# Routed experts as plain float32 products of 64-row blocks, with each expert's weights loaded once through a ring of four

## The chip, the core and the metric

The kernel runs on one core of one Trainium2 chip. The metric is the device time of one execution in microseconds. The engines named below are PE (TensorE, with PEld for its weight loads), ACT (ScalarE), DVE (VectorE), POOL (GpSimd) and SP (SyncE, which issues most DMAs); each has its own queue of instructions, and they meet only at semaphores.

## The reference, cut to what matters

512 tokens of 1024 columns run through a first block (an attention mixer, then a mixture of experts, then a norm) and a second block (another mixer and an MLP), all in float32. The change lies in the mixture of experts:

```python
scores = sigmoid(xf @ w_router)                       # 512 x 64
choice = scores + b_router                            # groups limited, then the 6 best experts of a token
gate = scores[chosen] / sum * 2.5
for each expert e, on the rows that chose it:
    hb = silu(xb @ w_exp_gate[e]) * (xb @ w_exp_up[e])   # 1024 -> 256
    yb = (hb @ w_exp_down[e]) * gate                     # 256 -> 1024
routed = sum of a token's six yb
shared = (silu(xf @ w_sh_gate) * (xf @ w_sh_up)) @ w_sh_down
```

There are 64 experts. One expert's three weight arrays take 1 MiB each. The 3072 assignments (512 tokens, six experts each) fall unevenly: counted from the reference's own routing on its inputs, an expert gets 5 to 126 of them, and 13 experts get more than 64.

## The kernel before, in words

The program is a sequence of stages, each with its own block of engine programs. Three of them matter here.

`ffn_front_stage` norms the tokens, stores them as rows in DRAM (`r["h"]`, L1475), turns them with TensorE (`turn`), multiplies by the router, picks experts with a long chain of small DVE operations (L1665 to L1724), counts rows for each expert with a triangular product (L1556), and builds lists that say which token stands in which row of which block. The rows of one expert are padded to whole blocks of 128; a block has one expert. DVE works out the expert of each block (L1707 to L1710) and SP carries that list through DRAM to a row on one partition (L1477 to L1485), from which it reads an expert's number into a register. The shared expert runs in the same stage: `shared_product` (four products of 8 tiles) and the down product at L1572 to L1580. `keep_busy` puts filler products on TensorE.

`expert_stage` loops over the blocks in use; four steps are written out, and the loop body holds four (`steps`, L1871). In step b:

- SP loads the weights of block b's expert into one of two places of `raw` (`gate_up` and `down`, L1911 to L1927), once the place's last contents have been split. Gate and up weights come in two halves A and B of 4 KB a partition and array, the down weights C in 8 KB a partition.
- ACT makes a high part in float32r of each piece (`high`, L2062), DVE the low part (`low`, L2107, in `low_part`, L108). Both go to one of four places, `parts`.
- POOL gathers the next block's rows into `xg` (L1971) and scatters results to `y_rows` (L1982); it copies the index column first (L1967, L1978).
- TensorE turns the rows (`turn_rows`, L2007), and multiplies. `split_product` (L99) makes one float32 product of three float32r products, high by high, high by low and low by high. A block has 24 such products of 512 columns for gate and up, 12 for down.
- ACT applies silu (L2096), DVE multiplies by the up half (L2135), TensorE turns the hidden rows (L2047), and TensorE's `down` runs one step later. ACT copies y (`copy_y`, L2083).

`combine_stage` loads each token's six rows of y again (`load_expert_rows`, L1797), six loads ahead of the two norm gains and six behind them, sums them with the gates (token tile 0 on DVE, the others with diagonal products on TensorE, L2213), adds them to x, and applies two norms, of which the first needs `gain` (L2302) and the second `gain2` (L2305).

Of the kernel before, what the change touches and what calls it, by code (L numbers as in the profile page):

```python
# [43 lines left out]
BLOCKS = S * TOPK // P + E  # L44
# [1323 lines left out]
def ffn_front_stage(g, io, hT, swp, r):  # L1368


# [6 lines left out]
    NB = BLOCKS + 4  # L1377
    PAD = 8 * S
    DOWN_BANK = [0, 2, 4, 6, 1, 3, 5, 7]
    HID_BANK = [1, 3, 5, 7]  # L1380
    LIST_BANK = 6
    raw, xg = r["raw"], r["xg"]
    with g.stage() as st:
        stat = g.sb("ffn_stat", [P, 3, NT], ctx=st)


        small = g.sb("router_rows_hidden", [P, 2 * D], F32R, ctx=st)
        coded = g.sb("coded_blocks", [P, 2, TOPK, 2, NB], F32R, ctx=st)
        sums = g.sb("tri_ones", [P, 2, P], F32R, ctx=st)
        Ar = g.sb("assigned_parts", [P, NT + 1, E], F32R, ctx=st)  # L1390
        br = g.sb("brouter", [P, E], ctx=st)
# [11 lines left out]
        A = g.sb("assigned", [P, NT + 1, E], ctx=st)  # L1403
        cnt = g.sb("counts", [P, 5, E], ctx=st)
        row = g.sb("expert_row", [P, NT, E], ctx=st)
# [4 lines left out]
        be = g.sb("block_expert", [P, E + 2], ctx=st)  # L1410
        lists = g.sb("row_lists", [P, NB], I32, ctx=st)
        lists_f = g.sb("row_lists_f", [P, NB], ctx=st)

        h = raw[:, 0, 0:2, :].rearrange("p a n -> p (a n)").rearrange("p (t d) -> p t d", t=NT)
        w = raw[:, 0, 2, 0:KD * E].rearrange("p (k n) -> p k n", k=KD)
        tmp = raw[:, 0, 2, KD * E:KD * E + NT * TOPK * E].rearrange("p (a e) -> p a e", e=E)

        sw = raw[:, 1]
        blocks = xg.rearrange("p u d -> p (u d)")[:, 0:2 * TOPK * NB].rearrange("p (i k b) -> p i k b", i=2, k=TOPK)
        wp = small[:, 0:2 * KD * E].rearrange("p (a k n) -> p a k n", a=2, k=KD)  # L1420
        rows_hot = small[:, 0:2 * TOPK * P].rearrange("p (i k q) -> p i k q", i=2, k=TOPK)
        hidp = small.rearrange("p (a m s) -> p a m s", a=2, m=2)
        gain = g.mod[:, 0:D]
        shared = g.mod[:, 0:4 * D].rearrange("p (t d) -> p t d", t=NT)
        shift, scale = (g.mod[:, i * D:(i + 1) * D] for i in (3, 4))

        hid = scale.rearrange("p (i s) -> p i s", i=2)
        gate_tmp = scale[:, 0:2 * TOPK * E].rearrange("p (a e) -> p a e", e=E)
# [5 lines left out]
        s_hi = g.sem("ffn_high_ready")  # L1434
        s_lo = g.sem("ffn_low_ready")
        s_hst = g.sem("ffn_h_stored")
        s_sw = [g.sem(f"shared_weights_loaded{i}") for i in range(3)]
        s_swh = g.sem("shared_high_ready")
        s_swl = g.sem("shared_low_ready")
# [3 lines left out]
        s_hh = g.sem("shared_hidden_high_ready")  # L1443
        s_hl = g.sem("shared_hidden_low_ready")
        s_dn = g.sem("shared_down_ready")
        s_wr = g.sem("wrouter_loaded")
        s_wp = g.sem("wrouter_parts_ready")
        s_ld = g.sem("route_loads")
        s_rt = g.sem("router_product_ready")
# [12 lines left out]
        s_bes = g.sem("block_experts_stored")  # L1462
# [3 lines left out]
        def _(sp):  # L1466
            sp.dma_start(gain, bcast_rows(io["g_ffn_norm"], D)).then_inc(s_gain, 16)
            sp.dma_start(w, io["w_router"][0].rearrange("(k p) n -> p k n", p=P)).then_inc(s_wr, 16)
            sp.dma_start(br[:], bcast_rows(io["b_router"], E)).then_inc(s_ld, 16)
            for i, key in enumerate(("w_sh_gate", "w_sh_up", "w_sh_down")):  # L1470
# [7 lines left out]
            sp.wait_ge(s_bes, 16)  # L1478
            sp.dma_start(r["be_row"][:], r["be_dram"].rearrange("b a -> a b")).then_inc(s_bes, 16)
# [3 lines left out]
            sp.wait_ge(s_wp, 2)  # L1483
            sp.wait_ge(s_cr, 1)
            sp.wait_ge(s_bes, 32)  # L1485
            fetch_gate_up(sp, io, r, 0)
            fetch_down(sp, io, r, 0)

            sp.wait_ge(s_swl, 3)
            fetch_gate_up(sp, io, r, 1)  # L1490
# [13 lines left out]
        def _(pe):  # L1504
# [59 lines left out]
            for t in range(NT):  # L1564
                list_rows(t)
# [2017 lines left out]
```

## Time and profile before

| | us |
|---|---|
| median of 3 runs | 2053.2 |
| lowest and highest run | 2051.46, 2054.91 |
| span of the profiled execution | 2048.1 |
| TensorE busy in the span | 1875.5 (92%) |
| DVE busy | 1287.6 (63%) |
| ACT busy | 1028.1 (50%) |
| POOL busy | 660.0 (32%) |

All times in the rows further down are microseconds from the span's start, or nanoseconds where a column says so. Busy time of TensorE is the time in which some product is under way, with ends that are modelled; the products overlap in it. A plain float32 product leaves two records in the trace, a float32r product or a transpose leaves one. The DMA share is the time that packets took over the time of 16 DMA engines, so it can pass 1 a little where packets of two queues overlap.

### The profile page before, as it was taken

What the parts mean: (1) busy time and instruction counts of PE and PEld (TensorE: products, weight loads), DVE (VectorE), ACT (ScalarE), POOL (GpSimd) and SP (SyncE); (2) the same over time, 40 slices, a digit from 0 to 9 for tenths busy, and PEclk for the clock granted to TensorE, in tenths of its full rate; (3) what the DMA queues carried; (4) which work ended last, traced back from release to release, by engine and by line L of the source; (5) the groups of instructions that cost most, each with busy time, mean ns of one, the idle gap of its engine ahead of it and who ended that gap; (6) DMA issues with size and microseconds to landing.
All of it is one profiled execution on the core that took longest, in us unless ns stands there. A gap on an engine that the chain in (4) does not pass through costs nothing. (4 is left out here: it accounts for less than half of the span.)

```text
span 2048.1 us, 28547 instructions
## 1 busy us (share of the span) xinstructions
PE 1875.5 (92%) x8812; PEld 1462.0 (71%) x8814; DVE 1287.6 (63%) x1494; ACT 1028.1 (50%) x1359; POOL 660.0 (32%) x526
## 2 busy tenths in 40 slices
PE   7988998997989999999999956899798879999999
PEld 3774665677868888888888834676465558888887
DVE  4673664446879999999999955564556652333332
ACT  3222444422258888888888833453655432222221
POOL 0896991000026666666666612110011100000000
PEclk9999999998889999999999977998899979999999
DMA  8755552123269999999999954332110023231321
GB/s 303 187 165 165 152 140 66 56 93 119 103 221 367 377 388 370 382 383 379 379 369 371 364 221 125 85 83 58 42 37 21 11 65 111 86 119 62 103 91 73
DMA packets 162992, 373.42 MB, mean 182 GB/s; under 512 B 35611, under 2 KB 72810, under 8 KB 154466
## 3 DMA queue, kind: packets, MB, share of 16 engines
q1 hardware_dynamic: 143954, 328.48, 46.0%
q0 software_dynamic: 18960, 43.91, 6.9%
q8 instruction: 48, 0.79, 0.2%
q14 instruction: 30, 0.25, 0.0%
HBM read 356.19 MB, written 29.23 MB: 188 GB/s over the span
## 5 line engine op out<-in xcount | busy, mean ns | idle before, releaser
L108 DVE TENSOR_TENSOR split_low_half<-exp_raw,split_low_half 128x2048 fp32r<-128x2048 f32 x101 | 230.1, 2290 | 32.7 <-ACT split_low_half L2071 32.7
L108 DVE TENSOR_TENSOR split_high_half<-exp_raw,split_high_half 128x2048 fp32r<-128x2048 f32 x96 | 218.6, 2290 | 27.3 <-ACT split_high_half L2071 27.2
L2071 ACT CAST split_low_half<-exp_raw 128x2048 fp32r<-128x2048 f32 x98 | 186.4, 1917 | 23.9 <-PEq L85 18.5
L102 PE MATMUL ps<-split_low_half,xgT 128*128 128x512 f32 x768 | 188.6, 399 | 3.4 <-DVE xgT L108 3.2
L102 PE MATMUL ps<-split_high_half,xgT 128*128 128x512 f32 x768 | 187.8, 397 | 1.1 <-issue 1.1
L2071 ACT CAST split_high_half<-exp_raw 128x2048 fp32r<-128x2048 f32 x96 | 182.5, 1917 | 2.5 <-PE ps L102 2.2
L102 PE MATMUL ps<-h4T,w_up_parts 128*128 128x512 f32 x768 | 176.8, 393 | 4.1 <-DVE w_up_parts L108 4.1
L102 PE MATMUL ps<-w_down_parts,hidden_parts 128*128 128x512 f32 x768 | 174.4, 390 | 0.0
L102 PEld LDWEIGHTS ps<-h4T,w_up_parts 128*128 128x128 f32 x768 | 146.0, 190 | 34.8 <-ACT w_up_parts L162 4.4
L1971 POOL DMA_INDIRECT xg<-h_rows,row_index x63 | 133.4, 2117 | 109.8 <-issue 82.5
L102 PEld LDWEIGHTS ps<-split_low_half,xgT 128*128 128x128 f32 x768 | 144.2, 191 | 34.4 <-issue 4.0
L102 PE MATMUL ps<-split_low_half,w_parts 128*128 128x512 f32 (+1 forms) x576 | 156.7, 427 | 9.9 <-DVE normed L3130 5.1
L102 PEld LDWEIGHTS ps<-w_down_parts,hidden_parts 128*128 128x128 f32 x768 | 144.2, 188 | 29.8
L102 PEld LDWEIGHTS ps<-split_high_half,xgT 128*128 128x128 f32 x768 | 143.2, 190 | 30.3 <-issue 1.2
L102 PEld LDWEIGHTS ps<-split_low_half,w_parts 128*128 128x128 f32 (+1 forms) x576 | 112.6, 200 | 44.2 <-issue 13.3
L1978 POOL COPY out_index<-row_asg_cols 128x1 uint32 x64 | 136.7, 2136 | 11.1 <-ACT exp_y L2083 11.0
L1982 POOL DMA_INDIRECT y_rows<-exp_y,out_index x64 | 86.4, 1350 | 110.0 <-PE ps L2007 61.4
L102 PE MATMUL ps<-h1T,mix_parts 128*128 128x512 f32 x384 | 104.8, 412 | 6.1 <-DVE mix_parts L108 6.1
L108 DVE TENSOR_TENSOR w_up_parts<-w_up_raw,w_up_parts 128x2048 fp32r<-128x2048 f32 (+1 forms) x19 | 36.9, 1954 | 110.3 <-ACT w_up_parts L167 108.9
L108 DVE TENSOR_TENSOR w_down_parts<-w_down_raw,w_down_parts 128x2048 fp32r<-128x2048 f32 (+1 forms) x19 | 36.8, 1954 | 106.7 <-ACT w_down_parts L167 106.7
L2690 POOL TENSOR_SCALAR sb_sums<-mod 128x1280 f32<-128x1280 f32 x6 | 20.7, 3449 | 255.0 <-ACT mod L3029 255.0
L102 PE MATMUL ps<-split_high_half,exp_hT 128*128 128x512 f32 x384 | 97.9, 405 | 2.8 <-DVE exp_hT L108 2.8
(453 smaller groups left out, 3564.6 us busy)
## 6 DMA issues: line engine op xcount, KB each, us to landing
exp_raw<-in_w_exp_gate SPq DMA_DIRECT2D x130, 512.0 KB, 6.2
exp_raw<-in_w_exp_up SPq DMA_DIRECT2D x130, 512.0 KB, 9.9
exp_raw<-in_w_exp_down SPq DMA_DIRECT2D x64, 1024.0 KB, 9.8
w_up_raw<-in_w_up SPq DMA_DIRECT2D x15, 1024.0 KB, 5.2
w_down_raw<-in_w_down SPq DMA_DIRECT2D x15, 1024.0 KB, 5.1
xg<-in_w_in SPq DMA_DIRECT2D x42, 256.0 KB, 3.3
gate_cols<-in_w_mod POOLq DMA_DIRECT2D x18, 512.0 KB, 4.6
exp_raw<-y_rows SPq DMA_DIRECT2D x9, 1024.0 KB, 14.2
```

The source lines that it names most:

```text
L102: mm = nc.tensor.matmul(out, left[a], right[b], start=start and i == 0, stop=stop and i == 2)
L108: return nc.vector.tensor_tensor(dst, x, high.bitcast(F32), ALU.subtract)
L1971: pool.indirect_dma_start(xg[0:n, u % 2, :], None, r["h"], bass.IndirectOffsetOnAxis(ap=idx[0:n, u % 2:u % 2 + 1], axis=0), bounds_check=S ...
L1978: nc.gpsimd.tensor_copy(oidx[:, u % 2:u % 2 + 1], r["row_asg_cols"][:, bass.ds(b - 4, 1)]).then_inc(s_oi, 1)
L1982: pool.indirect_dma_start(r["y"], bass.IndirectOffsetOnAxis(ap=oidx[0:n, u % 2:u % 2 + 1], axis=0), y[0:n, u % 2, :], None, bounds_check=T ...
L2071: nc.scalar.copy(dst, src).then_inc(s_hi[kind], 1)
L2690: nc.gpsimd.tensor_scalar(su[:], z[:], 0.0, None, ALU.max).then_inc(s_br, 1)
```

## The change

- A block has 64 rows in place of 128 (`ROWS`), and an expert with up to 128 rows has up to two blocks. The list of blocks grows to 112 with 8 spare columns. Every expert has at least one block.
- The 128 partitions of a gathered block hold its 64 rows twice: rows 0 to 63 hold the first 512 columns of the tokens, rows 64 to 127 the last 512. Rows of DRAM are addressed as half rows of 2 KB, for the gather and for the scatter.
- All expert products are plain float32 with 64 stationary columns. Two go to the two halves of the array's columns in turn: out partitions 0 to 63 and 64 to 127. Gate and up take 16 products of 256 columns a block, down takes 4 of 512. There are four turns of the rows and one of the hidden rows.
- The split into high and low parts is gone in the loop and in the front stage. In its place DVE copies pieces A and B, and ACT copies piece C, from the ring to fixed places (`work`), once for each block, at an address that a register gives.
- SP loads each of the 64 experts once, in order, through a ring of four places, `SLOTS`. It no longer reads the block list. It relays each landing to a counter (`s_land`) for which ACT and DVE wait, and it loads expert e + 4 once all blocks of expert e are copied (`r["ends"]`). Experts 0 and 1 are loaded from the start of the front stage, 2 after the last shared down product, 3 right after it.
- The expert of each block reaches its row through a TensorE transpose in place of DRAM. The index columns are copied by DVE in place of POOL, four blocks ahead, into four places.
- The router and the shared expert are plain float32, straight from the loaded weights. All `keep_busy` calls but the first (32 fillers) are gone.
- The combination loads all twelve pairs of y rows ahead of the gains, into the four places of the ring.

```diff
-BLOCKS = S * TOPK // P + E
+ROWS = 64
+BLOCKS = S * TOPK // ROWS + E
+NB = BLOCKS + 8
+SLOTS = 4
...
 def ffn_front_stage, sync
+            fetch_expert(sp, io, r, 0, 0)
             for t in range(NT):
                 sp.wait_ge(s_h, t + 1)
                 sp.dma_start(r["h"][t * P:t * P + P, :], h[:, t, :]).then_inc(s_hst, 16)
-            sp.wait_ge(s_be, 1)
-            sp.dma_start(r["be_dram"], r["be_col"][0:NB, :]).then_inc(s_bes, 16)
...
+            fetch_expert(sp, io, r, 1, 1)
+
+            sp.wait_ge(s_sp, 4)
+            sp.wait_ge(s_dn, 8)
+            fetch_expert(sp, io, r, 2, 2)
...
+            fetch_expert(sp, io, r, 3, 3)
...
 def ffn_front_stage, tensor
                 for k in range(KD):
                     c = k * F + (m % 2) * P
-                    mm = split_product(nc, g.ps[:, HID_BANK[m], :], [swp[:, m // 2, a, c:c + P] for a in range(2)],
-                                       parts_of(hT, k), k == 0, k == KD - 1)
+                    mm = nc.tensor.matmul(g.ps[:, HID_BANK[m], :], sw[:, m // 2, c:c + P], hT[:, k, :],
+                                          start=k == 0, stop=k == KD - 1)
...
             shared_product(2)
+            pe.wait_ge(s_be, 1)
+            nc.tensor.transpose(g.ps[:, EXPERT_BANK, 0:P], be[:], g.ident[:]).then_inc(s_et, 1)
+            list_rows(0)
+            list_rows(1)
             shared_product(3)
-            keep_busy(g, 8, 4)
-            for t in range(NT):
-                list_rows(t)
-            keep_busy(g, 10, 4)
+            list_rows(2)
+            list_rows(3)
...
+def fetch_expert(sp, io, r, e, place):
     for half in range(2):
         for j, key in enumerate(("w_exp_gate", "w_exp_up")):
+            src = io[key][0].rearrange("e (h p k) f -> e h p (k f)", h=2, p=P)
+            sp.dma_start(r["raw"][:, place, half, 1024 * j:1024 * j + 1024],
+                         src[bass.ds(e, 1), half].rearrange("a p n -> p (a n)")).then_inc(r["s_raw"][half][place], 16)
+    src = io["w_exp_down"][0].rearrange("e (k p) n -> e p k n", p=P)
+    sp.dma_start(r["raw"][:, place, 2, :].rearrange("p (k n) -> p k n", k=2),
+                 src[bass.ds(e, 1)].rearrange("a p k n -> p (a k) n")).then_inc(r["s_raw"][2][place], 16)
...
 def expert_stage, sync
+        def relay(kind, u, i):
+            sp.wait_ge(s_raw[kind][u], (32, 32, 16)[kind] * (i + 1))
+            sp.sem_inc(s_land[kind], 1)
+
+        def expert(u, i, last):
+            relay(C, u, i)
+            if not (last and u == SLOTS - 1):
+                for kind in (A, B):
+                    relay(kind, (u + 1) % SLOTS, i + (u + 1) // SLOTS)
+            if not last:
+                blocks = sp.value_load(r["ends"][0:1, bass.ds(SLOTS * i + u, 1)], min_val=1, max_val=BLOCKS)
+                for kind in (A, B, C):
+                    sp.wait_ge(s_cp[kind], blocks)
+                fetch_expert(sp, io, r, SLOTS * i + u + SLOTS, u)
...
 def expert_stage, gpsimd
-            pool.wait_ge(s_xt, b - 1)
-            nc.gpsimd.tensor_copy(idx[:, u % 2:u % 2 + 1], r["row_tok"][:, bass.ds(b, 1)]).then_inc(s_i, 1)
-            pool.wait_ge(s_i, b - 1)
+            pool.wait_ge(s_i, b - 3)
             pool.sem_inc(s_seen, 1)
...
 def expert_stage, tensor
+            for k in range(4):
+                tr = nc.tensor.transpose(g.ps[:, u % 2, k * P:k * P + P], xg[:, u % 4, k::4], g.ident[:])
...
+            pe.wait_ge(s_cp[half], b + 1)
+            w = work[:, place(half, u), :].rearrange("p (j k f) -> p j k f", j=2, k=4)
+            for k in range(4):
+                for n in range(2):
+                    mm = nc.tensor.matmul(g.ps[ROWS * n:ROWS * n + ROWS, 2 + u % 2, 0:F],
+                                          xT[:, u % 2, k, ROWS * half:ROWS * half + ROWS], w[:, :, k, P * n:P * n + P],
+                                          start=half == 0 and k == 0, stop=half == 1 and k == 3)
...
+            for k in range(2):
+                for n in range(2):
+                    c = k * D + n * 512
+                    mm = nc.tensor.matmul(g.ps[ROWS * n:ROWS * n + ROWS, 5 + o, :], hT[:, o, ROWS * k:ROWS * k + ROWS],
+                                          work[:, place(C, u - 1), c:c + 512], start=k == 0, stop=k == 1)
...
 def expert_stage, scalar
+        def down_weights(b, u, first):
+            e = expert_of(act, b)
+            act.wait_ge(s_land[C], e + 1)
+            free_place(act, C, b, first, u)
+            nc.scalar.copy(work[:, place(C, u), :], piece_at(C, e)).then_inc(s_cp[C], 1)
...
+            rows_copied(b + 1, u + 1)
             if not start:
                 copy_y(b, u, first, i)
+            down_weights(b, u, first)
             act.wait_ge(s_ht, b + 1)
+            nc.scalar.copy(hT[:, u % 2, :], g.ps[:, 4, 0:P]).then_inc(s_hc, 1)
...
 def expert_stage, vector
+            e = expert_of(dve, b)
+            for kind in (A, B):
+                dve.wait_ge(s_land[kind], e + 1)
+                free_place(dve, kind, b, first, u)
+                nc.vector.tensor_copy(work[:, place(kind, u), :], piece_at(kind, e)).then_inc(s_cp[kind], 1)
...
 def combine_stage, sync
-        for t in range(2, NT):
-            for j in range(PAIRS):
-                if t >= 3:
-                    sp.wait_ge(s_used, min(TOPK, 2 * j + 2))
-                load_expert_rows(sp, r, yk[t % 3], t, j, s_y[t % 3][j])
```

## Rows read from the trace of the kernel before

**Rows 1.** Busy by stretch: PE, PEld, DVE, ACT, POOL; clock, DMA share, GB/s.
```profile
483.00:576.00 93.00, 80.80 (x425) 73.15 (x425) 71.89 (x169) 27.37 (x61) 4.08 (x3) 0.81 0.38 137
554.00:585.00 31.00, 22.90 (x94) 19.01 (x93) 25.65 (x39) 8.14 (x9) 6.49 (x4) 0.72 0.52 201
576.00:1201.00 625.00, 610.73 (x2952) 512.07 (x2952) 555.62 (x387) 526.01 (x456) 373.92 (x254) 0.98 0.97 355
700.00:1000.00 300.00, 299.78 (x1469) 252.04 (x1468) 273.94 (x193) 258.55 (x223) 190.14 (x128) 1.00 1.02 380
```

**Rows 2.** Who waited for whom, 600 to 1180: total, times, longest.
```profile
ACT split_low_half L2071 <- DMA exp_raw<-in_w_exp_up: 1.3, 2, 0.7
```

**Rows 3.** Waits of SP's own queue, 600 to 1180.
```profile
SPq L1916 <- DVE split_low_half L108: 85.5, 60, 1.7
```

**Rows 4.** Groups by line and shape, whole run: busy us, mean ns, idle before.
```profile
L102 PE MATMUL ps<-split_low_half,xgT 128*128 128x512 f32 x768 | 188.6, 399 | 3.4 <-DVE xgT L108 3.2 <-issue 0.2
L2071 ACT CAST split_low_half<-exp_raw 128x2048 fp32r<-128x2048 f32 x98 | 186.4, 1917 | 23.9 <-PEq L85 18.5 <-PE ps L102 4.1 <-DMA exp_raw<-in_w_exp_up 1.3
...
L330 DVE COPY cond<-silu_c 128x1024 f32<-128x1024 f32 x1 | 0.7, 694 | 0.0
...
L3007 ACT COPY soft_pt<-ps 128x512 f32<-128x512 f32 x12 | 7.0, 579 | 11.1 <-PE ps L2758 11.1
```

**Rows 5.** DMA view, 640 to 1170: queue, packets, MB, share of 16 engines.
```profile
DMA packets 50823, 199.26 MB, mean 376 GB/s; under 512 B 9365, under 2 KB 9365, under 8 KB 43644
...
q1 hardware_dynamic: 40453, 176.71, 89.4%
q0 software_dynamic: 10368, 22.53, 12.0%
```

**Rows 6.** DMA view of 0 to 40, then of 1205 to 1238.
```profile
DMA packets 7176, 14.48 MB, mean 362 GB/s; under 512 B 1551, under 2 KB 2136, under 8 KB 6920
...
DMA packets 4291, 13.39 MB, mean 406 GB/s; under 512 B 246, under 2 KB 1137, under 8 KB 4290
```

**Rows 7.** Timeline of PE, line L1127: start, us, what, records.
```profile
242.75 0.66 PE L1127 MATMUL ps<-win_raw,v_mla 128*64 128x128 f32 x8
...
254.12 1.10 PE L1127 MATMUL ps<-win_raw,v_mla 128*64 128x128 f32 x16
```

**Rows 8.** Timeline of PE, line L2776, one half of the columns.
```profile
1444.02 0.87 PE L2776 MATMUL ps<-soft_pt,values 128*64 128x128 f32 x6
...
1458.82 1.09 PE L2776 MATMUL ps<-soft_pt,values 128*64 128x128 f32 x8
```

**Rows 9.** Timeline of the front stage: last score, shared down, first weight split.
```profile
520.03 0.22 ACT L1602 ACTIVATE scores<-ps 128x64 f32<-128x64 f32 x1 [4.90 <-PE ps L102]
...
560.05 11.45 PE L102 MATMUL ps<-split_low_half,router_rows_hidden 128*128 128x512 f32 x48
...
575.91 1.90 ACT L2071 CAST split_low_half<-exp_raw 128x2048 fp32r<-128x2048 f32 x1 [18.48 <-PEq L85]
```

**Rows 10.** Timeline of the loop's end and of the combination.
```profile
1185.61 1.91 ACT L2071 CAST split_high_half<-exp_raw 128x2048 fp32r<-128x2048 f32 x1
...
1190.42 4.60 PE L102 MATMUL ps<-split_high_half,exp_hT 128*128 128x512 f32 x12 [2.77 <-DVE exp_hT L108]
...
1198.24 0.91 POOL L1982 DMA_INDIRECT y_rows<-exp_y,out_index  x1 [1.74 <-issue]
...
1201.44 3.38 SPq L1797 DMA_DIRECT2D exp_raw<-y_rows  x6
1204.86 1.28 SPq L2194 DMA_DIRECT2D final_gain<-in_g_final  x1
...
1220.99 1.29 DVE L2302 SCALAR_TENSOR_TENSOR x<-x,final_stat,final_gain 128x1024 f32<-128x1024 f32 x1 [0.99 <-DMA final_gain<-in_g_final]
...
1227.33 7.13 PE L2213 MATMUL ps<-yk,gate_diagonals 128*128 128x512 f32 x16 [0.22 <-DMA yk<-y_rows]
...
1235.56 1.29 DVE L108 TENSOR_TENSOR split_low_half<-ps,split_low_half 128x512 fp32r<-128x512 f32 x2 [4.56 <-ACT split_low_half L2248]
```

More of the change, by code:

```diff
@@ L1577, in _ @@
                     col = k * D + n * 512
-                    mm = split_product(nc, g.ps[:, DOWN_BANK[c], :], parts_of(hidp, k, t * P, t * P + P),
-                                       [swp[:, 0, a, col:col + 512] for a in range(2)], k == 0, k == 1)
+                    mm = nc.tensor.matmul(g.ps[:, DOWN_BANK[c], :], hid[:, k, t * P:t * P + P], sw[:, 2, col:col + 512],
+                                          start=k == 0, stop=k == 1)
                 mm.then_inc(s_dn, 1)
@@ L1654, in _ @@
             link(v.reciprocal(stat[:, 1, :], stat[:, 2, :]))
-            rows(0)
-            rows(1)
-            rows_low(0)
-            rows(2)
-            rows_low(1)
-            rows(3)
-            rows_low(2)
-            rows_low(3)
-            shared_low(0)
+            for t in range(NT):
+                rows(t)
             dve.wait_ge(s_ld, 16)
@@ L1900, in used_blocks, with expert_of, piece_at @@
     def used_blocks(eng):
-        return eng.value_load(r["n_col"][0:1, 0:1], min_val=24, max_val=BLOCKS)
-    def rhs_of(piece, k):
-        return [parts[piece][:, a, k * 512:k * 512 + 512] for a in range(2)]
+        return eng.value_load(r["ends"][0:1, E - 1:E], min_val=E, max_val=BLOCKS)
+    def expert_of(eng, b):
+        return eng.value_load(r["be_row"][0:1, bass.ds(b, 1)], min_val=0, max_val=E - 1)
+    def piece_at(kind, e):
+        return raw[:, bass.ds(e & (SLOTS - 1), 1), kind, :].rearrange("p a n -> p (a n)")
@@ L1946, in _ @@
+        used = used_blocks(sp)
+        relay(A, 0, 0)
+        relay(B, 0, 0)
+        with sp.Fori(0, E // SLOTS - 1) as i:
+            for u in range(SLOTS):
+                expert(u, i, False)
+        for u in range(SLOTS):
+            expert(u, E // SLOTS - 1, True)
+        sp.wait_ge(s_cp[A], used + 1)
+        sp.wait_ge(s_cp[B], used + 1)
+        sp.wait_ge(s_cp[C], used)
         sp.wait_ge(s_st[0], ((used + 1) >> 1) * 16)
         sp.wait_ge(s_st[1], (used >> 1) * 16)
-        for t in range(2):
+        for t in range(NT):
@@ L2019, in down @@
         def down(b, u, first, i=0):
-            pe.wait_ge(s_hi[C], b)
-            pe.wait_ge(s_lo[C], b)
-            pe.wait_ge(s_hh, b)
-            pe.wait_ge(s_hl, b)
-            if not (first and u == 1):
-                pe.wait_ge(s_y, b - 1)
-            for n in range(2):
-                for k in range(2):
-                    mm = split_product(nc, g.ps[:, 5 + n, :], [hT[:, (u - 1) % 2, a, k, :] for a in range(2)],
-                                       rhs_of(place(C, u - 1), 2 * k + n), k == 0, k == 1)
+            pe.wait_ge(s_cp[C], b)
@@ L2031, in down @@
+            pe.wait_ge(s_hc, b)
+            if not (first and u < 3):
+                pe.wait_ge(s_y, b - 2)
+            o = (u - 1) % 2
+            for k in range(2):
[3 more added lines that the diff above has]
+                                          work[:, place(C, u - 1), c:c + 512], start=k == 0, stop=k == 1)
             mm.then_inc(s_piece, 1)
@@ L2041, in step @@
             gate_up(b, u, 1)
-            turn_rows(b + 1, u + 1, i, False)
+            turn_rows(b + 1, u + 1, i, first and u == 0)
             if not (first and u == 0):
@@ L2168, in combine_stage @@
     s_gain = [g.sem(f"final_gain_loaded{i}") for i in range(2)]
-    s_y = r["s_y"] + [[g.sem(f"y_loaded2{j}") for j in range(PAIRS)]]
+    s_y = r["s_y"]
     s_diag = g.sem("gate_diagonals_ready")
@@ L2360, in moe_and_mixer2 @@
-            r["row_asg_cols"] = g.sb("row_asg_cols", [P, BLOCKS + 4], U32, ctx=c)
-            r["row_tok"] = g.sb("row_tok", [P, BLOCKS + 4], I32, ctx=c)
-            r["s_raw"] = [[nc.alloc_semaphore(f"expert_{n}_loaded{i}") for i in range(2)]
+            r["raw"] = g.sb("exp_raw", [P, SLOTS, 3, 2048], ctx=c)
+            r["y_buf"] = g.sb("exp_y", [P, 2, D // 2], ctx=c)
+            r["be_row"] = g.sb("be_row", [1, NB], I32, ctx=c)
+            r["ends"] = g.sb("expert_ends", [P, E], I32, ctx=c)
```

406 lines of the change are left out of this document (127 added, 279 removed).

## The prediction

> **What bounds the kernel now.** I began with busy times by stretch. The change touches three: the routed front of the mixture (483 to 576 us), the expert loop (576 to 1201) and the combination (1201 to about 1264). The loop is 30% of the span, and in it TensorE is busy 610.7 of 625 us and the DMA engines 0.97 [rows 1]; inside it, from 700 to 1000 us, the two stand at 299.8 of 300 and 1.02, with 380 GB/s moved. Both are full, so I asked who waits for whom. ACT, the first reader of a loaded weight, waits 1.3 us for DMA in 580 us [rows 2], while SP, which issues the loads, waits 85.5 us on one line alone for DVE to free a buffer [rows 3]. So TensorE sets the pace (64 blocks from 576 [rows 9] to 1195 [rows 10], 9.7 us a block), and DMA just keeps up: it is a second limit that lies directly under the first. That is the whole case: taking work from TensorE, ACT and DVE can win only what lies between the two, plus what the new loading order adds.
>
> The profiled span is 2048.1 us and the median of the runs 2053.2 us (2051.46 to 2054.91), so some 5 us lie around the span. I sum differences on the span and take them off the median.
>
> **Blocks.** Counted from the reference's own routing on its inputs, 13 experts have over 64 rows, none over 128 and none has no row. So 64 blocks become 64 + 13 = 77, and the loads stay 64 experts: before, one expert's weights a block (and one extra load), after, one an expert.
>
> **TensorE per block.** Before: 36 products of 512 columns a block at 188.6 / 768 = 0.246 us [rows 4], 8.8 us, and ten transposes. After: plain float32, where one product leaves two records. A 512-column product costs 2 x 7.13 / 16 = 0.89 us in the combination [rows 10]. Whether two 64-column products in the two halves run at once decides everything. The trace has it: at L1127 values of two heads alternate between the halves; 8 and 16 records of 128 columns take 0.66 and 1.10 us [rows 7], 0.22 us for every four records, that is for one product in each half. L2776 works on one half only: 6 and 8 records take 0.87 and 1.09 us [rows 8], 0.22 us for one product. So the pair costs what one costs. Per block: eight pairs of 256 columns at 0.44 and two of 512 at 0.89, 5.3 us; five transposes at 0.11 (a record of [rows 8]), 0.55; two changes between halves and the whole array. No row prices that change by itself: the 8 records of [rows 7] take 0.66 where the slope gives 0.44, so filling and change are at most 0.22 us together, at least nothing; I take 0.15. Together 6.2 us.
>
> **ACT, DVE and POOL per block.** ACT copies the down weights (1.92 [rows 4]), the turned rows and y (0.58 each by the 128x512 copy of [rows 4]) and does two small operations, about 0.7 together by the 128x512 row as an upper bound: 3.8 us. New is that it reads a register from SBUF ahead of the weight copy; the nearest row is POOL's gap of 1.74 us, where it reads one and branches [rows 10], so 0 to 1.74. Behind that load are queued the weight copy and the hidden copy, for which the down product waits: down 1.8, y 0.6, register 0 to 1.7, copy 1.9, hidden copy 0.4 make a loop of 4.7 to 6.4 us. DVE copies 2048 columns twice; the 1024-column copy took 0.69 [rows 4], so at most 1.4 each, and with the product, two index copies and a register 3.5 to 5.2 us. POOL loses its two index copies to DVE. So a block takes 6.2 to 6.5 us and 77 take 477 to 500, against 619.
>
> **DMA becomes the bound.** The loop has 64 x 3.146 = 201.3 MB of weights. Two experts are fetched during the front, where the share is 0.38 [rows 1]; the third waits for the shared expert's last product. So 62 x 3.146 = 195.0 MB remain, and 3072 rows of 4 KB in and out, 25.2 MB: 220.2 MB. Rows move in pieces of 2 KB now, weights all in 4 KB. The rate: 380 GB/s inside the loop [rows 1], 376 over 640 to 1170, at which the two queues' shares add up to 1.01 [rows 5]. The ends are 362 at the kernel's start, with mostly 2 KB pieces and no indirect transfer, and 406 in the combination, 4 KB pieces with no indirect transfer [rows 6]. I take 380, the same mixture of queues: 579 us, with 608 and 542 as ends. The ring of four keeps at least two experts on order while a slot is freed, so I charge no gap. Against 579, compute of 500 and some 10 us of start is hidden, and has 579 / 77 = 7.5 us a block before it shows.
>
> The Trainium skill, "DMA: Bandwidth & Descriptors", Specifications, gives an HBM limit per core of about 358 GB/s, which speaks against this change: 220.2 MB would take 615 us and nearly all the gain would be gone. The 380 and 406 of the two stretches stand against it, so it has no place in the sum; a rate near it is the rival of slower transfers, priced from rows.
>
> **The front.** Removed: the low parts on DVE, the high parts on ACT, a third of the router's records, and the trip of the block list through DRAM. Added: plain products on TensorE, where one (0.89) replaces three of 0.246, so the 16 shared down products take 14.2 us for 11.45 [rows 9]; wider block lists on DVE (120 for 92 columns); the wait of the list product for the expert row. The last score comes at 520.0, and from there a chain of small DVE operations is unchanged. I expect the last score 8 us earlier, 1 us less in the counting, and 5 given back on TensorE, some of it at the lower clock since filler products go: the last shared product ends near 567.5 instead of 571.5. Bounds: 0 to 10 us earlier. The four gathers at its end (POOL) replace two and lie beside those products.
>
> **Start and end of the loop.** Loads run from 567.5, the last lands at 567.5 + 579 = 1146.5. Then the old tail from the last weight copy to the loads of y, 1185.6 to 1201.4, 15.8 us [rows 10], shortened by a down product of 1.8 for 4.6 and a y copy of half the width, 13 us: y is asked for at 1159.5 instead of 1201.4, 41.9 earlier.
>
> **The combination.** All twelve loads of y (12.6 MB) now go out ahead of the final gain, where six did. Before, the gain was issued at 1204.9, and DVE's first use was at 1221.0, after a wait for it [rows 10]. After, 12.6 MB and the gain at 406 GB/s land 32.5 us after the first load for 19.5 before. TensorE's sums hid part of this: DVE's first low part came at 1235.6, 34.1 us in, after them; after, gain, two norms and a turn put it about 41 us in. Cost 7 us (0 to 13).
>
> **Sum.** -41.9 + 7 = -35 on 2053.2: 2018 us. With the rate between 370 and 395 GB/s, 2000 to 2035.
>
> **Rivals.**
> Faster transfers: with ACT and DVE reading less and weights in long runs, the rate reaches the combination's 406: 37 us less, 1981. Against it: indirect transfers stay, in twice as many pieces.
> Slower transfers: 2 KB pieces bring the rate to 362: 29 us more, 2047.
> The clock (the slower end): TensorE waits for weights in every expert, its granted clock falls between 2.4 and 1.2 GHz, and compute becomes the bound. With TensorE at 22.9 of 31 us busy, the clock was 0.72 from 554 to 585 [rows 1]. At 0.72 a block takes 5.85 / 0.72 + 0.3 = 8.4 us, 77 take 649, and with start and tail y is asked for at 1239: 38 + 7 later, 2098. It decides from (1201.4 - 7 - 13 - 571) / 77 = 7.9 us a block on. Against it: once compute is late TensorE no longer waits, and busy it has 1.00 [rows 1]; so it should settle near 7.5 to 8. The Trainium skill, "TensorE: Matmul & The Clock Gate", The HAM clock gate, has the half rate as the default that activity lifts; the 0.72 agrees, and no run here shows the clock under just these gaps.
> The halves don't run together (the change doesn't do what it says): a block takes 5.3 more, 11.5 us, 77 take 886, 2340. The records of [rows 7] speak against it, though at 128 columns, not 256 or 512.
>
> **How the numbers follow.** Chances: forecast 0.52; faster transfers 0.15; slower transfers 0.12; clock or another compute bound over 7.5 us 0.17, a fifth of it still faster; halves one after the other 0.04. A measurement of this kernel tells about 0.2%, 4 us. Faster: 0.52 + 0.15 + most of 0.12, and 0.03, 0.77; same 0.05; slower 0.18. The range takes in most of the fast and slow transfers and a mild compute bound: 1985 to 2060.
>
> **What would show it.** Right: ACT and DVE idle before weight copies with DMA as releaser; DMA share about 1 from 570 to 1146; TensorE busy about 480 of 590; one 64-column product per 0.44 us at 512 columns on average; the first DVE norm waiting for the gain. Wrong: SP waiting for copies while DMA falls under 0.9 (compute bound); records of both halves in single file; a granted clock under 0.9 in the loop; a rate off 370 to 395.

## The result and the profile after

The changed kernel takes 2062.0 us (median of 6 runs, 2057.7 to 2065.5) and the kernel before 2052.8 us (6 runs, 2051.1 to 2055.4): a ratio of 1.0051, 95% interval 1.0029 to 1.0074. The forecast was 2018 us, with a range up to 2060. The change costs 9 us where it should have brought 35, and the time is just above the range. All medians and ratios here leave out three executions that ran far longer than the rest: one of the kernel before (10347 us) and two of `gains_early` (2310 and 3172 us).

First busy time by stretch (columns as in [rows 1]) of the changed kernel:

```profile
576.00:700.00 124.00, 107.70 (x698) 57.25 (x696) 44.40 (x80) 56.03 (x79) 40.21 (x31) 0.93 0.84 317
...
700.00:1000.00 300.00, 261.68 (x1669) 143.94 (x1667) 102.89 (x184) 130.77 (x185) 90.13 (x75) 0.92 0.93 358
...
1000.00:1100.00 100.00, 85.68 (x536) 48.84 (x532) 30.81 (x56) 40.22 (x58) 25.36 (x23) 0.90 1.02 401
1100.00:1200.00 100.00, 86.58 (x549) 47.26 (x549) 35.79 (x65) 44.64 (x62) 28.71 (x23) 0.92 0.72 277
```

In [rows 1] TensorE and DMA were both full from 700 to 1000. Now neither is: TensorE 262 of 300, DMA 0.93, ACT 131 and DVE 103 (259 and 274 before). When no engine is full, the time lies in waits between them. These are the waits from 570 to 1240 (total, times, longest), of DVE:

```profile
DVE work_places L2009 <- SPq L1846: 261.5, 42, 9.1
```

and of SP's own queue:

```profile
SPq L1856 <- ACT work_places L1976: 372.2, 60, 14.2
...
SPq L1846 <- DMA exp_raw<-in_w_exp_up: 5.1, 2, 2.6
SPq L1846 <- DMA exp_raw<-in_w_exp_down: 2.5, 1, 2.5
```

L1846 is the relay: SP adds one to the counter `s_land` when a weight has landed. DVE waits 261.5 us for the relay, and SP at the relay waits 7.6 us for landings in all (5.1 and 2.5). So DVE waits for weights that are there. SP spends 372 us in front of L1856, the wait until all blocks of an expert are copied, which stands in its program ahead of the next relay. In the kernel before, ACT waited for DMA itself [rows 2], and SP's wait was the one for a free buffer [rows 3]; no signal went through SP.

The steps tell it most plainly. From one silu (L1993) to the next there are 76 steps: 49 take 6.4 us (the first of them 5.0), and 27 take 10.4 to 13.1, together 128 us over 6.41 each. One late step and the ordinary one behind it, from the timeline (start, duration; idle before and its releaser in brackets):

```profile
1042.42 1.90 ACT L1976 COPY work_places<-exp_raw 128x2048 f32 x1 [0.33 <-issue]
...
1044.56 0.34 SPq L1734 DMA_DIRECT2D exp_raw<-in_w_exp_gate  x1
...
1045.29 0.28 ACT L1993 ACTIVATE exp_sig<-ps 128x128 f32<-128x128 f32 x1 [0.80 <-PE ps L1923]
...
1045.86 1.94 PE L1938 MATMUL ps<-work_places,exp_hT 128*64 128x512 f32 x8
...
1046.47 0.40 SPq L1737 DMA_DIRECT2D exp_raw<-in_w_exp_down  x1
...
1047.40 2.37 DVE L2009 COPY work_places<-exp_raw 128x2048 f32 x2 [7.80 <-SPq L1846]
...
1049.69 0.27 DVE L2019 TENSOR_TENSOR exp_h<-ps,exp_sig 128x128 f32<-128x128 f32 x1
...
1050.02 0.33 PE L1954 MATMUL ps<-ident,exp_h 128*128 128x128 f32 x1 [2.22 <-DVE exp_h L2019]
...
1050.70 5.16 PE L1923 MATMUL ps<-work_places,xgT 128*64 128x256 f32 x32 [0.36 <-issue]
...
1055.90 0.28 ACT L1993 ACTIVATE exp_sig<-ps 128x128 f32<-128x128 f32 x1 [4.98 <-PE ps L1923]
...
1056.48 1.94 PE L1938 MATMUL ps<-work_places,exp_hT 128*64 128x512 f32 x8
...
1058.35 0.33 PE L1954 MATMUL ps<-ident,exp_h 128*128 128x128 f32 x1
...
1058.60 3.67 PE L1923 MATMUL ps<-work_places,xgT 128*64 128x256 f32 x32
```

Read it as one chain. ACT's copy of the down weights ends at 1044.32. SP waited for that, and issues the five loads of a later expert from 1044.56 to 1046.87. Only then come the relays, and DVE's copies for the next block start at 1047.40, though the load of those weights was issued from 1027.42 on and a load of this kind landed 8.6 us after its issue in the median from 1000 to 1100. DVE works in program order, and the product of the present block (L2019) stands behind these copies. Its input was ready at 1045.57; it starts at 1049.69. TensorE, done at 1047.80, waits 2.22 us, and after that its 32 records take 5.16 us instead of 3.67. The granted clock says why:

```profile
1050.00:1056.00 6.00, 5.62 (x34) 3.57 (x35) 1.65 (x4) 1.02 (x3) 1.67 (x2) 0.72 1.03 414
1056.00:1062.00 6.00, 6.00 (x45) 3.19 (x44) 1.12 (x4) 3.42 (x5) 1.69 (x2) 1.00 1.02 408
```

From 1050 to 1056, behind the wait, it is 0.72, a mixture of 1.2 and 2.4 GHz; from 1056 to 1062, with TensorE busy without a gap, 1.00. So this step of 10.6 us (1045.29 to 1055.90) is 6.4, plus 2.3 for the late hidden rows (4.16 us from the start of the down product to their transpose, against 1.87), 0.4 until the next product starts (0.68 against 0.25), and 1.5 at the lower clock.

The other two stages of the changed kernel: the front's last score, its last shared products and DVE's first copy (with SP's last issue of the front between), and the combination's loads with the first norm that waits for the gain, and the first weight split of the next stage.

```profile
508.12 0.22 ACT L1584 ACTIVATE scores<-ps 128x64 f32<-128x64 f32 x1 [1.12 <-PE ps L1507]
...
547.78 13.90 PE L1567 MATMUL ps<-exp_raw,mod 128*128 128x512 f32 x32
...
566.58 0.49 SPq L1737 DMA_DIRECT2D exp_raw<-in_w_exp_down  x1
...
569.98 3.50 DVE L2009 COPY work_places<-exp_raw 128x2048 f32 x3 [5.14 <-SPq L1846]
...
1205.15 17.17 SPq L1744 DMA_DIRECT2D exp_raw<-y_rows  x12
...
1240.01 1.28 DVE L2180 SCALAR_TENSOR_TENSOR x<-x,final_stat,final_gain 128x1024 f32<-128x1024 f32 x1 [16.21 <-DMA final_gain<-in_g_final]
...
1277.19 1.99 ACT L2822 CAST w_parts<-xg 128x1024 fp32r<-128x1024 f32 x2 [1.71 <-PEq L88]
```

and that first weight split in the kernel before:

```profile
1264.70 1.99 ACT L2948 CAST w_parts<-xg 128x1024 fp32r<-128x1024 f32 x2 [1.73 <-PEq L85]
```

The ledger in the two profiled executions (2048.1 and 2063.7 us, 15.6 apart): the first weight copy 5.9 us earlier (575.91 in [rows 9], 569.98 now), the loop from there to the first load of y 9.6 us longer (625.5 and 635.2), the combination up to the next stage's first split 8.8 us longer (1264.70 less 1201.44 = 63.3, and 72.0). That is 12.5; the remaining 3.1 lies in later stages, which the change doesn't touch. The profiled execution of the changed kernel was the slowest of its six, so the two profiles lie further apart than the medians (9 us).

### The profile page after: what moved, and what is told of

The parts are those of the page before. It is cut to its first block and busy times, and to the rows that moved or that the text cites. A ratio compares the mean times of both kernels' runs of the same rounds, so it can differ in the third digit from the quotient of the medians.

```text
span 2063.7 us, 29262 instructions
## 1 busy us (share of the span) xinstructions
PE 1814.0 (88%) x9192; PEld 1226.4 (59%) x9192; DVE 935.8 (45%) x1480; ACT 772.1 (37%) x1290; POOL 473.7 (23%) x424
## 5 line engine op out<-in xcount | busy, mean ns | idle before, releaser
L2009 DVE COPY work_places<-exp_raw 128x2048 f32 x156 | 189.9, 1243 | 382.9 <-SPq L1846 261.5
L1923 PE MATMUL ps<-work_places,xgT 128*64 128x256 f32 x2464 | 329.9, 427 | 11.2 <-issue 8.8
L1923 PEld LDWEIGHTS ps<-work_places,xgT 128*64 128x64 f32 x2464 | 208.7, 154 | 109.6 <-issue 38.1
L105 PE MATMUL ps<-mix_hT,w_parts 128*128 128x512 f32 (+1 forms) x576 | 159.8, 432 | 9.8 <-DVE normed L3004 5.0
L1976 ACT COPY work_places<-exp_raw 128x2048 f32 x77 | 146.4, 1901 | 25.4 <-issue 25.4
L1938 PE MATMUL ps<-work_places,exp_hT 128*64 128x512 f32 x616 | 150.8, 610 | 3.1 <-ACT exp_hT L1999 3.1
L105 PEld LDWEIGHTS ps<-mix_hT,w_parts 128*128 128x128 f32 (+1 forms) x576 | 113.1, 201 | 46.2 <-issue 13.9
L1884 POOL DMA_INDIRECT xg<-h_rows,row_index x74 | 88.8, 1200 | 47.7 <-DVE out_index L2022 26.4
L1993 ACT ACTIVATE exp_sig<-ps 128x128 f32<-128x128 f32 x77 | 21.4, 278 | 190.3 <-PE ps L1923 190.3
L105 PEld LDWEIGHTS ps<-h1T,mix_parts 128*128 128x128 f32 x384 | 70.0, 194 | 29.0 <-issue 8.2
L1984 ACT COPY exp_y<-ps 128x512 f32<-128x512 f32 x77 | 45.1, 586 | 107.7 <-PE ps L1938 107.7
```

What stands on the lines that cost most here:

```text
L105: mm = nc.tensor.matmul(out, left[a], right[b], start=start and i == 0, stop=stop and i == 2)
L1884: pool.indirect_dma_start(xg[:, u, :], None, h_halves, bass.IndirectOffsetOnAxis(ap=idx[:, u:u + 1], axis=0), bounds_check=2 * S - 1, oob_ ...
L1923: mm = nc.tensor.matmul(g.ps[ROWS * n:ROWS * n + ROWS, 2 + u % 2, 0:F], xT[:, u % 2, k, ROWS * half:ROWS * half + ROWS], w[:, :, k, P * n: ...
L1938: mm = nc.tensor.matmul(g.ps[ROWS * n:ROWS * n + ROWS, 5 + o, :], hT[:, o, ROWS * k:ROWS * k + ROWS], work[:, place(C, u - 1), c:c + 512], ...
L1976: nc.scalar.copy(work[:, place(C, u), :], piece_at(C, e)).then_inc(s_cp[C], 1)
L1984: nc.scalar.copy(y[:, o, :], g.ps[:, 5 + o, :]).then_inc(s_y, 1)
```

## The experiments

Theory S: SP's program order makes landed weights late. Theory D: the loop is at the limit of the transfers, as the DMA share of 1.02 from 1000 to 1100 suggests. Theory R: the ring of four is too short. All kernels below are the changed kernel with the edit that is shown. "Late" counts steps over 6.6 us in the profiled execution, with what they take over 6.41 in all; "y" is the start of the first load of y there.

| kernel | median us | ratio to before, 95% | late steps, us over | y |
|---|---|---|---|---|
| changed kernel | 2062.0 | 1.0029 to 1.0074 | 27, 128 | 1205.2 |
| relay_ahead | 2003.0 | 0.9718 to 0.9796 | 26, 67 | 1144.4 |
| relay_before_issue | 2004.4 | 0.9720 to 0.9797 | 40, 69 | 1145.4 |
| half_weights | 2081.9 | 1.0098 to 1.0180 | 27, 151 | 1225.5 |
| few_bytes | 2064.4 | 1.0036 to 1.0074 | 29, 124 | 1201.1 |
| ahead_few_bytes | 1932.8 | 0.9377 to 0.9455 | 0, 0 | 1073.9 |
| gains_early | 2053.3 | 0.9985 to 1.0031 | 27, 124 | 1196.6 |
| ahead_gains | 1997.2 | 0.9699 to 0.9750 | 27, 70 | 1146.6 |
| one_half | 2331.0 | 1.1309 to 1.1402 | 75 of 11.6, one of 8.5 | 1474.2 |
| ahead_down_long | 1994.0 | 0.9686 to 0.9769 | 25, 62 | 1136.4 |
| ahead_more_copies | 2004.2 | 0.9756 to 0.9807 | 27, 67 | 1146.0 |

### Relays one expert earlier

```diff
-            relay(C, u, i)
             if not (last and u == SLOTS - 1):
+                relay(C, (u + 1) % SLOTS, i + (u + 1) // SLOTS)
+            if not (last and u >= SLOTS - 2):
                 for kind in (A, B):
-                    relay(kind, (u + 1) % SLOTS, i + (u + 1) // SLOTS)
+                    relay(kind, (u + 2) % SLOTS, i + (u + 2) // SLOTS)
             if not last:
                 ... wait for the copies of expert 4 i + u, issue its place's next load
... (ahead of the loop: the relays of expert 0, and A and B of expert 1)
```

> Three theories for the loop of the changed kernel, in which 49 of 76 steps take 6.4 us and 27 take 10.4 to 13.1, 128 us over in all. Theory S (the queue of SP): SP passes on the landing of a weight to the counter that DVE and ACT wait for, but in its program this stands behind the wait for the copies of the expert before and behind five DMA issues, so weights that have long landed are copied late. Theory D (transfers): DMA share 1.02 from 1000 to 1100 us says that the loop already runs at the rate of the transfers, and late steps are steps that wait for them. Theory R (ring): four places are too few. Here SP passes landings on one expert earlier, ahead of the wait for copies and the issues; nothing else changes. S expects the late steps to go until the transfers are the limit: 220.2 MB at 390 to 400 GB/s from 562 us and a tail of 13 give loads of y at 1125 to 1140 in place of 1205, a time of 1982 to 1997. D and R expect 2055 to 2065, as the transfers and the places are the same.

2003.0 us: 59 us less, with the same transfers and the same ring. D and R as the cause of the changed kernel's time fall. Two stretches:

```profile
580.00:700.00 120.00, 119.97 (x846) 63.82 (x840) 54.90 (x94) 65.19 (x94) 48.65 (x37) 1.00 0.97 377
...
700.00:1000.00 300.00, 267.56 (x1802) 147.87 (x1800) 113.55 (x196) 140.83 (x200) 100.55 (x80) 0.97 1.02 402
```

and SP's waits from 570 to 1140:

```profile
SPq L1846 <- DMA exp_raw<-in_w_exp_up: 259.4, 105, 3.8
SPq L1857 <- ACT work_places L1979: 66.2, 20, 9.8
```

The pair of waits has changed places: at the relay SP now waits 259.4 us for landings (5.1 before) and 66 instead of 372 us for copies. Up to 700 us TensorE is full, and DMA moves 377 GB/s; from 700 on DMA is full, at 402. This is the loop that the prediction described. S had expected 1982 to 1997, from 390 to 400 GB/s all the way; the 26 steps that are still late begin at 724 us, in the part where transfers set the pace.

The gain over the changed kernel doesn't come evenly. Counted by steps, relay_ahead leads by 55 us after 52 of the 76 (993 us in the changed kernel) and by 56 after 68 (1131 us). Between these the changed kernel moves as much as relay_ahead (401 GB/s from 1000 to 1100), so there the late relay, that of the step read above too, costs nothing beyond what the transfers take anyway; its price is paid before.

### Relays behind the wait, but ahead of the issues

```diff
             if not last:
                 ... wait for the copies of expert 4 i + u
+            ... the relays, as in relay_ahead
             if not last:
                 fetch_expert(sp, io, r, SLOTS * i + u + SLOTS, u)
```

> As the kernel that passes landings on earlier, but they keep their place behind the wait for the copies and go only ahead of the five issues, which take SP about 2.5 us (1044.56 to 1046.87). S in its narrow form (the issues alone make the landing late): the copy at 1047.40 would begin near 1044.9, and the hidden rows, late by 2.3 us, would be in time, so nearly all late steps go: 1985 to 2020. S in its wide form (the wait itself is too late): late steps shrink to half, 2020 to 2045. D and R: 2055 to 2065.

2004.4 us, the same as with relays ahead of the wait. So the narrow form holds: it is the five issues, 2.3 to 3.0 us on SP in the late steps, that made the relay cost so much, and the wait itself adds little. Up to 720 us, where transfers set no pace yet, delays of 0.4 to 1.0 us remain in six steps; that the transfer-bound part then hides them is not shown by a run of its own. The Trainium skill, "DMA: Bandwidth & Descriptors", Issuing engines are not separate DMA queues, says that the sequencer's time to start a DMA is usually small beside the DMA itself. The trace agrees, some 2.6 us for 3.1 MB, which take about 8 us at 402 GB/s; but it was in the way of the relay, and that cost 59 us.

### Fewer bytes, twice, and once more with earlier relays

```diff
-    sp.dma_start(r["raw"][:, place, ...], src[bass.ds(e, 1), ...])
+    sp.dma_start(r["raw"][0:64, place, ...], src[bass.ds(e, 1), 0:64, ...])          # half_weights
+    sp.dma_start(... [:, :, 0:64], src[bass.ds(e, 1), :, :, 0:64] ...)               # few_bytes, down weights only
```

> The changed kernel with half the bytes for each weight loaded in the loop (60 experts): 64 of 128 partitions are loaded, so the other half holds old weights and the result is another; the number of DMAs, the waits and all the copies and products stay. S expects the time to stay within 10 us of 2062, because no late step waits for bytes. D expects 119 MB in place of 214 MB to end the late steps, with compute of 77 times 6.41 us as the limit: y asked for near 1075, a time of about 1930. R expects a gain of the same kind, because landings come sooner after a place is free.

2081.9 us, 20 more than the changed kernel, where S had within 10 of it. The run didn't separate the theories as meant: the bytes halved, but the packets took nearly the same time. It shows something else. The stretch from 1000 to 1100 us:

```profile
1000.00:1100.00 100.00, 80.03 (x475) 48.18 (x473) 29.96 (x55) 39.36 (x57) 25.92 (x22) 0.87 0.94 205
```

and the first and the last of five issues on SP's timeline:

```profile
790.42 0.52 SPq L1734 DMA_DIRECT2D exp_raw<-in_w_exp_gate  x1
...
792.99 0.64 SPq L1737 DMA_DIRECT2D exp_raw<-in_w_exp_down  x1
```

The five issues take SP 3.2 us here (790.42 to 793.63), and 3.2 in the mean of the 27 late steps, in place of 2.6 in the changed kernel; the 27 late steps are 0.85 us longer each (151 us in place of 128). SP waits 6.5 us for landings at the relay, so the weights are there in this kernel too. More time on SP goes with longer late steps, a dose of the suspected cause, though not the one that was planned; 0.6 us more came out as 0.85, and where the rest comes from is open.

> The changed kernel (relays in their place) with a load of the down weights in the loop that brings 64 of 1024 columns, so the result is another; every DMA, wait, copy and product stays. Half the partitions halved the bytes but not the time of the packets (DMA share 0.94 at 205 GB/s), so that run said little of theory D. Here all 128 partitions stay and an expert brings 2.16 MB in place of 3.15. S: 27 late steps as before, time within 8 us of 2062. D: the late steps go, 1930 to 1960.

2064.4 us, 29 late steps. A third of the bytes less changes nothing: D falls a second time, now with a cut that did thin out the transfers, also from 1000 to 1100 us, where the changed kernel had 1.02 and 401 GB/s:

```profile
700.00:1000.00 300.00, 261.85 (x1679) 146.68 (x1677) 104.73 (x186) 130.90 (x185) 89.71 (x74) 0.92 0.73 263
1000.00:1100.00 100.00, 83.73 (x522) 45.27 (x519) 30.40 (x59) 42.34 (x60) 26.86 (x24) 0.90 0.79 285
```

> The same cut of bytes on the kernel that passes landings on one expert earlier. Its late steps (26, 67 us over 6.41 in all) begin where the slack between landing and copy is 0.3 us, so they should be waits for transfers: 62 times 2.16 MB and 25.2 MB of rows at 402 GB/s are 396 us, less than 77 times 6.41 = 494. If so, nearly all steps take 6.4 us and the time falls by about 65 us, to 1935 to 1942. If SP's queue still holds them, it stays within 20 us of 2003.

1932.8 us, just under the 1935 to 1942 that were expected, and no late step at all. The row of 600 to 1050:

```profile
600.00:1050.00 450.00, 450.00 (x3160) 238.21 (x3160) 209.37 (x353) 246.81 (x352) 187.25 (x141) 1.00 0.90 331
```

TensorE is busy 450.00 of 450 at clock 1.00. So compute alone is 6.41 us a step, and in relay_ahead the transfers are the limit, 70 us above compute in y.

### One half of the array's columns

```diff
-    nc.tensor.matmul(g.ps[ROWS * n:ROWS * n + ROWS, 2 + u % 2, 0:F], ...)
+    nc.tensor.matmul(g.ps[0:ROWS, 7 if n else 2 + u % 2, 0:F], ...)
... (the start and stop flags to match, and the same for the down product)
```

> The changed kernel with all expert products on the first half of the array's columns: the second product of each pair goes to the same 64 columns and another bank, so its result is left out. Same number of products, same columns, same waits. The step of the prediction that the halves run at once says that the pairs fall apart: 8 pairs of 256 columns at 0.46 us and two of 512 at 0.97 cost 5.6 us more a step, 12.0 in place of 6.41; 77 steps are 924 us without late steps, y is asked for near 1500, a time near 2350. If the halves run one after the other as it is, nothing changes: 2062.

2331.0 us. A stretch of TensorE's timeline:

```profile
802.09 7.12 PE L1923 MATMUL ps<-work_places,xgT 128*64 128x256 f32 x32
809.14 0.75 PE L1915 MATMUL ps<-ident,xg 128*128 128x128 f32 x4
809.82 3.65 PE L1938 MATMUL ps<-work_places,exp_hT 128*64 128x512 f32 x8
```

7.12 and 3.65 us against 3.67 and 1.94: on two halves a pair costs what one product costs. The step is 11.6 us, 5.2 more than 6.41 where 5.6 were expected, and no step is longer than that: with compute this slow the relay is always in time.

### The order of the gains

```diff
 def expert_stage, sync
-        for t in range(NT):
-            for j in range(TOPK // 2):
-                load_expert_rows(sp, r, rows_place(r, t), t, j, r["s_y"][t][j])
+        for j in range(TOPK // 2):
+            load_expert_rows(sp, r, rows_place(r, 0), 0, j, r["s_y"][0][j])
...
 def combine_stage, sync
         ... issue the two gains
+        for t in range(1, NT):
+            for j in range(PAIRS):
+                load_expert_rows(sp, r, yk[t], t, j, s_y[t][j])
```

> The changed kernel with the two norm gains issued behind the first three loads of y in place of all twelve. The prediction put the cost of the order at 7 us (0 to 13); the traces show 72.0 us from the first load of y to the first weight split of the next stage, against 63.3 before, and a wait of 16.2 us for the gain. If that wait is the cause, the time falls by 5 to 10 us, to 2052 to 2057. If the sums of TensorE, which start at 1218 and have 60 records, set the end of the stage anyway, it stays within 3 us of 2062.

2053.3 us, 9 less; from the first load of y to the next stage's first split it is 67.2 us (1196.63 to 1263.81) in place of 72.0. So the stretch that was changed gives 4.8 us in the profiles; the rest lies ahead of it (y at 1196.6 and 1205.2), where the two kernels don't differ. The ratio to before includes 1: a loss is no longer seen.

> Landings passed on one expert earlier, and the two gains issued behind the first three loads of y. The two effects lie in different stages and should add: 2003 less 6 to 8 us, 1995 to 1997.

1997.2 us, 5.8 less than relay_ahead; the stretch is 65.6 us (1146.59 to 1212.14) in place of 73.2. The first norm in the two kernels, relay_ahead first:

```profile
1179.23 1.28 DVE L2183 SCALAR_TENSOR_TENSOR x<-x,final_stat,final_gain 128x1024 f32<-128x1024 f32 x1 [16.22 <-DMA final_gain<-in_g_final]
```

```profile
1165.23 1.28 DVE L2185 SCALAR_TENSOR_TENSOR x<-x,final_stat,final_gain 128x1024 f32<-128x1024 f32 x1
```

The wait of 16.2 us is gone. This kernel leaves nothing out, and it beats the kernel before by 2.7% and the changed one by some 3%.

### Why 402 GB/s and not 380

```diff
-    src = io["w_exp_down"][0].rearrange("e (k p) n -> e p k n", p=P)
+    src = io["w_exp_down"][0].rearrange("e (p k) n -> e p (k n)", p=P)               # ahead_down_long
```
```diff
+            nc.vector.tensor_copy(g.mod[...2048 columns], g.x[...])                  # ahead_more_copies, in each step
+            nc.scalar.copy(g.mod[...1024 columns], g.x[...])
```

> Where the transfers are the limit, the kernel with earlier relays moves 402 GB/s (700 to 1000 us) against 380 in the kernel before, both at a DMA share of 1.02, and the whole difference lies in the packets of SP's queue: 0.882 of 300 us for 99.3 MB before, 0.892 for 106.1 MB. One thing that differs there is the run of the down weights: 8 KB a partition before, two of 4 KB now. This is the kernel with earlier relays and the down weights in one run of 8 KB a partition, as before (rows come in another order, so the result is another). If the run is the cause, the rate falls to 380 to 385 in that stretch and the time rises by 20 to 30 us, to 2023 to 2033. If it is something else, such as the smaller traffic of ACT and DVE, it stays at 400 to 404 GB/s and within 5 us of 2003.

> The other side of the same question: the kernel with earlier relays, and in each step one more copy of 2048 columns on DVE (1.24 us) and one of 1024 on ACT, from x to a place that nobody reads. Between 700 and 1000 us ACT and DVE were busy 141 and 114 us there, against 274 and 259 in the kernel before. If their traffic is what brought 380 GB/s there against 402 here, these copies, some 60 us of DVE and 40 of ACT in 300, should bring the rate to about 390 to 396, and the time up by 8 to 17 us, beside what the copies delay in the steps that compute sets. If the rate stays at 400 to 404, the traffic isn't the cause, and a rise would have to show as longer steps of their own.

The rate stayed in both. From 700 to 1000 us, with the long run first, then with more copies:

```profile
700.00:1000.00 300.00, 268.02 (x1794) 149.06 (x1792) 114.41 (x199) 142.04 (x202) 100.42 (x82) 0.97 1.01 404
```

```profile
700.00:1000.00 300.00, 268.98 (x1804) 150.20 (x1804) 158.55 (x239) 176.20 (x241) 100.49 (x81) 0.97 1.02 402
```

Neither the run of the down weights nor this much more traffic of DVE and ACT (45 and 35 us busy more) costs rate. That is some three tenths of what the two were busy more in the kernel before (274 for DVE and 259 for ACT, which the expectation has the other way round). The long run is if anything better (1994 us, where within 5 of 2003 was expected, but the intervals overlap). What held the kernel before at 380 stays open; row pieces of 4 KB in place of 2 KB and the rest of its traffic were not tried.

## Why the prediction was wrong

**What bounds the kernel now.** Right: TensorE, with DMA as a second limit directly beneath. When the change took TensorE's load away and the relays were in time, DMA was the limit (relay_ahead).

**Blocks.** Right: 77 steps, 32 records of gate and up in each (2464 in the profile).

**TensorE per block.** Forecast 6.2 to 6.5 us, measured 6.41. The halves run at once, as [rows 7, 8] had it, also at 256 and 512 columns (one_half).

**ACT, DVE and POOL per block.** Here the working went astray in kind. It added up busy times (3.8 us for ACT, 3.5 to 5.2 for DVE) and followed one loop through ACT and TensorE's down product (4.7 to 6.4). As bounds the sums hold: from 700 to 1000 us, at 8.1 us a step, ACT is busy 3.5 us and DVE 2.8 a step. But it didn't follow a new path through four queues: ACT's copy, SP's wait, five issues and relay, DVE's copies and then its product, TensorE's transpose. Each is short, and they stand in a row. The text names what is queued behind ACT's register load; it doesn't name what is queued behind DVE's new wait for `s_land` (the present block's product), nor what stands ahead of the relay in SP's program.

**DMA becomes the bound.** The failing step is the sentence "The ring of four keeps at least two experts on order while a slot is freed, so I charge no gap". The ring did hold landed weights; nobody was told. The missing term is the relay behind five issues in SP's program: 128 us of late steps against compute, of which 59 us come back when the relays pass the issues; from then on the transfers set the pace. The rate was off too, to the good: 402 GB/s where 380 was taken and 395 was the end of the likely case. The 406 of the combination [rows 6] was the nearer row; of the two reasons given for it, one (long runs) was tried and fell, and of the other (less reading by ACT and DVE) a part was tried and showed nothing. The limit of 358 GB/s that the prediction cites from the Trainium skill doesn't bind this core: 402 was held for 300 us. The Trainium skill, "Perfetto Trace Analysis", Roofline, gives a reason: 358 is the share when both cores of a pair draw, and one core alone may take more. The kernel runs on one core, and no run here has a second one at work.

**The front.** Forecast 4 us earlier (0 to 10): the shared down products end at 561.7 in place of 571.5, 9.8 earlier. The last score came 11.9 us earlier, not 8, and the down products took 13.9 (14.2 forecast). But the loop starts only 5.9 earlier: SP's ten issues of experts 2 and 3 (561.76 to 567.07) now stand between the last product and DVE's first copy (569.98, behind a wait for SP), which the sum left out.

**Start and end of the loop.** From the last down copy (1194.93) to y (1205.15) it is 10.2 us. But the forecast set its 13 behind the last landing, and there they are too few. In relay_ahead the transfers fade out around 1120, and the last copy that waits for a landing starts at 1123.99:

```profile
1110.00:1120.00 10.00, 8.81 (x69) 5.29 (x67) 2.77 (x5) 5.80 (x8) 3.43 (x3) 1.00 0.88 345
1120.00:1130.00 10.00, 7.17 (x54) 4.32 (x52) 5.10 (x7) 3.52 (x5) 1.00 (x1) 1.00 0.12 49
```

```profile
1123.99 1.23 DVE L2012 COPY work_places<-exp_raw 128x2048 f32 x1 [2.01 <-SPq L1846]
```

y is asked for at 1144.4, 20 us behind that copy: 13.9 us from the last silu (1130.53) and most of a step before it, which the sum left out. That y still comes 15 us before the 1159.5 of the forecast is owed to loads that end some 22 us sooner, by the earlier front and the faster rate; two misses offset each other in part.

**The combination.** Forecast 7 us (0 to 13), measured 8.8, and 5 to 8 us of the stretch come back when the gains move forward.

**The rivals.** The outcome belongs to "another compute bound over 7.5 us" (0.17): the mean step was 8.1 us, just beyond the 7.9 that the text gives as the point of decision, and half of its sign came ("SP waiting for copies", but DMA at 0.93 and 357 GB/s from 570 to 1146 us, not under 0.9). Its mechanism was not what happened: TensorE was busy 262 us of 300, and in the step read above the clock takes 1.5 us of 4.2 and follows the wait; it doesn't start it. That the time came out near this rival is luck. Faster transfers came true in relay_ahead (402 GB/s); in the changed kernel they were hidden behind the relay. Slower transfers did not come: where DMA was full, it moved 401. Halves in single file did not come either.

## What to carry to other kernels

When a queue both issues transfers and passes on that they have landed, walk its program in order and ask of each signal what stands ahead of it: five issues of some 0.5 us ahead of a relay cost 59 us here, while the weights lay ready. An engine's busy time is no price for a step; the price is the longest path around the loop, through every queue that it crosses. If the engines and DMA are all under full after a change, look for a pair of waits in which A waits for B's signal and B doesn't wait for the event.

## What the runs showed of the hardware

Loads into 64 of 128 partitions moved 205 GB/s at a DMA share of 0.94, where loads into all 128 moved 401 at 1.02: half the bytes in nearly the same time of the engines. The Trainium skill, "SBUF — State Buffer", Door 1: The DMA port swizzle, states that partitions 0 to 63 reach half of the ports; the run agrees. Five issues also took SP 3.2 us in place of 2.6 in the mean of the late steps; the cause of that is open.

A wait of 2.2 us on TensorE between two blocks was enough for the next product to run in part at 1.2 GHz: 5.16 us in place of 3.67, at a granted clock of 0.72 over 1050 to 1056. In relay_ahead, too, 32 records took 5.36 us behind a wait of 2.92. In these two places a wait cost the time waited and 1.5 and 1.7 us more.
